# Mixture-of-experts blocks: gate and up columns side by side in one 512-column product, inner weights in pieces by halves of the rows

## The chip, the cores and the metric

The kernel runs on one core of one Trainium2 chip. The metric is device time in microseconds (us), the median over several executions. One further execution is recorded by the hardware profiler; its trace is what is read here.

## The reference

The input x is 2048 tokens of 1024 float32 numbers. A layer of convolution and state-space mixing comes first, and then a mixture of experts, cut here to what the change touches:

```
h = rms_norm(x, g_ffn)
# each token picks 1 of 4 groups, and in it 2 of 8 experts, with two gate values
for each block of 128 (token, expert) assignments of one expert e:
    hid = silu(xblk @ w_gate[e]) * (xblk @ w_up[e])      # 128x1024 @ 1024x512, twice
    y   = hid @ w_down[e]                                # 128x512  @ 512x1024
    out[token] += gate * y
```

There are 32 experts; each has its assignments padded to whole blocks of 128. The last step is a normalisation of the sum.

## The kernel before

The stages run one after the other: input projection, convolution and state space, mixing with the router, experts, final norm. The change lies in the experts' stage alone, in `ExpertWeights` and `experts`.

**Blocks.** The loops are dynamic: an outer one over the 32 experts e, an inner one over the blocks j of the expert (`over_blocks`, L1819 and the lines after it). With the inputs used there are 46 blocks. Each of the five engines runs its own copy of both loops and reads the counts from on-chip memory at each new expert. Every engine executes its instructions in program order; they are tied together by semaphores only.

**Weights.** Every product is made in three parts, for float32-like precision on TensorE: with a high and a low part of both operands, hi*hi + lo*hi + hi*lo. An expert's weights come in six pieces of 128x2048 (1 MB each). In the kernel before they are G0, U0 (gate and up for the first 256 hidden units, all 1024 rows), G1, U1 (the same for the other 256), D0, D1 (down). A piece is loaded by SyncE into `raw`, rounded by ScalarE into `hi` (`split_hi`, L1633), and subtracted by VectorE into `lo` (`split_lo`, L1637). Each of the three buffers holds one expert. The split of expert e + 1 is done during the last block of expert e (the `If(j == last - 1)` branch), each piece after the products that read the old one; the order is written out by hand in the two `body` functions of ScalarE and VectorE. In the last expert nothing is split, so 31 blocks hold a split.

**A block on TensorE** (`body` of the tensor engine), in order: `hidden` G0, U0, G1, each 8 row chunks of 3 products of 256 columns; `turn_hidden(b, 0)`, two transposes of the first half of the hidden values (L2045), which wait for VectorE's `join(b, 0)`; `hidden` U1; `turn_x(b + 1)`, eight transposes of the next block's input (L2029); `down(b, 0, 0)`, six products of 512 columns, which wait for the low part of the hidden values (`hid_low(b, 0)`, L1961); `turn_hidden(b, 1)`; three more `down`.

**Half k of the hidden values** goes through ScalarE `silu` (L1897), VectorE `join` (L1956, reads the up columns in PSUM), TensorE `turn_hidden`, ScalarE `hid_high` (L1901), VectorE `hid_low`. ScalarE's `scale_y` (L1906) takes the block's result out of PSUM, and GpSimd adds it to memory by an indirect DMA (L1879). Before `scale_y`, ScalarE waits for the block's slots `ids_s`, which GpSimd loads (L1873) once the scatter of the block before has landed.

In PSUM, gate half 0 and up half 1 share one bank (`p_g0u1`).

Of the kernel before, what the change touches and what calls it, by code (L numbers as in the profile page):

```python
# [13 lines left out]
P = 128  # L14
# [7 lines left out]
NE = NG * EPG  # L22
# [1586 lines left out]
G0, U0, G1, U1, D0, D1 = range(6)  # L1609


class ExpertWeights:
# [27 lines left out]
    def inner(self, part, u, c):  # L1640

        return part[:, u, c * 256:(c + 1) * 256]
# [130 lines left out]
def experts(nc, scratch, ident, routing, weights):  # L1773
# [7 lines left out]
    with ExitStack() as ctx:  # L1781
# [8 lines left out]
        p_g0u1, p_u0, p_g1, p_hid = ps("p_g0u1"), ps("p_u0"), ps("p_g1"), ps("p_hid")  # L1790
        p_gate = [p_g0u1[:, 0:H], p_g1[:, 0:H]]
        p_up = [p_u0[:, 0:H], p_g0u1[:, H:2 * H]]
# [17 lines left out]
        gate_done, up_done, sil_done, hid_done = (sem(n) for n in ("gate_done", "up_done", "sil_done", "hid_done"))  # L1810
# [78 lines left out]
        def _(act):  # L1889
# [5 lines left out]
            def silu(b, k):  # L1895
                act.wait_ge(gate_done, b * 2 + k + 1)
                nc.scalar.activation(sil[:, k * H:(k + 1) * H], p_gate[k], ACT.Silu).then_inc(sil_done, 1)  # L1897
# [17 lines left out]
            def body(b, e, j, last):  # L1915
                with act.If(j == last - 1):
                    silu(b, 0)
                    weights.split_hi(act, e + 1, G0)
                    act.wait_ge(up_done, b * 2 + 1)
                    weights.split_hi(act, e + 1, U0)  # L1920
                    silu(b, 1)
                    hid_high(b, 0)
                    weights.split_hi(act, e + 1, G1)
                    turn_x(b + 1)
                    hid_high(b, 1)
                    weights.split_hi(act, e + 1, U1)
                    act.wait_ge(ids_s_in, b * 16 + 16)
                    for i in range(2):
                        scale_y(b, i)
                    weights.split_hi(act, e + 1, D0)  # L1930
                    weights.split_hi(act, e + 1, D1)
                with act.Else():
                    silu(b, 0)
                    silu(b, 1)
                    hid_high(b, 0)
                    turn_x(b + 1)
                    hid_high(b, 1)
                    act.wait_ge(ids_s_in, b * 16 + 16)
                    for i in range(2):
                        scale_y(b, i)  # L1940
# [3 lines left out]
        def _(dve):  # L1944
# [8 lines left out]
            def join(b, k):  # L1953
                dve.wait_ge(sil_done, b * 2 + k + 1)
                dve.wait_ge(up_done, b * 2 + k + 1)
                V.tensor_tensor(hid[:, k * H:(k + 1) * H], p_up[k],  # L1956
# [47 lines left out]
            def body(b, e, j, last):  # L2004
                with dve.If(j == last - 1):
                    join(b, 0)
                    weights.split_lo(dve, V.tensor_tensor, e + 1, G0)
                    weights.split_lo(dve, V.tensor_tensor, e + 1, U0)
# [4 lines left out]
                    for u in (G1, U1, D0, D1):  # L2013
# [10 lines left out]
        def _(pe):  # L2024
# [7 lines left out]
            def hidden(out, e, u, done):  # L2032

                pe.wait_ge(w_lo, e * weights.PIECES + (u + 1))
                for c in range(KD):
                    w_hi, w_low = weights.inner(hi, u, c), weights.inner(lo, u, c)
                    nc.tensor.matmul(out, xh[:, c], w_hi, start=c == 0, stop=False)  # L2037
                    nc.tensor.matmul(out, xl[:, c], w_hi, start=False, stop=False)  # L2038
                    last_mm = nc.tensor.matmul(out, xh[:, c], w_low, start=False, stop=c == KD - 1)  # L2039
                last_mm.then_inc(done, 1)  # L2040
# [28 lines left out]
            def body(b, e, j, last):  # L2069
                pe.wait_ge(x_lo, b * 2 + 2)  # L2070
                wait(pe, hid_done, b * 2)
                hidden(p_gate[0], e, G0, gate_done)
                hidden(p_up[0], e, U0, up_done)
                hidden(p_gate[1], e, G1, gate_done)
                turn_hidden(b, 0)
                pe.wait_ge(sil_done, b * 2 + 1)
                hidden(p_up[1], e, U1, up_done)
# [104 lines left out]
```

## Time and profile before

| | |
|---|---|
| median of 3 runs | 1887.34 us (1884.49 to 1889.06) |
| the profiled execution's own time | 1895.12 us |
| its span, first to last instruction | 1893.7 us |
| mean granted TensorE clock | 0.924 |
| TensorE busy, share of the span | 1640.9 us, 87% |
| VectorE, ScalarE, GpSimd | 59%, 42%, 32% |

The span is 1.4 us shorter than the time of the same execution. Busy time of TensorE is a sum of modelled ends of pipelined instructions, so two starts that follow each other tell more than a duration does. PE stands for matmuls, PEld for the loads of the stationary operand, DVE for VectorE, ACT for ScalarE, POOL for GpSimd, SP for SyncE. A row of the timeline gives start, length, engine, line, what is written from what, the number of merged instructions, and in brackets the idle time of the engine before it and what ended it; "issue" is idle time that no shown wait explains.

### The profile page before, as it was taken

To read this page: it belongs to the slowest core of one execution; us is meant where nothing else is said; L and a number is where in the kernel's file an instruction comes from. 1 tells how busy PE (TensorE), PEld (TensorE's weight loads), DVE (VectorE), ACT (ScalarE), POOL (GpSimd) and SP (SyncE) were. 2 spreads that over 40 slices of the span, in tenths; PEclk is the share of its full clock that TensorE was granted. 3 is DMA by queue.
4 is the path that set the end of the run, shared out by engine and by line. 5 is a ranking of instruction groups with operands and counts; after the bars stand their busy time and mean duration, and the time that the engine had idled before them with its cause. 6 is when DMAs were issued, how large, how long until landed. Compare 5 with 4: busy or idle time off the path is not lost. (4 is left out here: it accounts for less than half of the span.)

```text
span 1893.7 us, 33245 instructions
## 1 busy us (share of the span) xinstructions
PE 1640.9 (87%) x11171; PEld 1500.2 (79%) x11172; DVE 1116.7 (59%) x1707; ACT 803.3 (42%) x1022; POOL 605.9 (32%) x882
## 2 busy tenths in 40 slices
PE   7699999688937999999269999999999999999970
PEld 7599999577827888888268999899999888989860
DVE  7845564244547566665617646654666886665546
ACT  3222221012245333342315646644665775665543
POOL 0776774222323336444311212121222121212120
PEclk9899999878968898989579999999999999999995
DMA  8544342498854224312539878885877999887749
GB/s 278 169 146 147 127 161 85 121 223 247 225 200 137 97 89 134 101 67 90 215 119 316 275 240 272 274 285 188 291 273 257 382 366 359 280 275 254 261 137 366
DMA packets 166974, 403.90 MB, mean 213 GB/s; under 512 B 67967, under 2 KB 103169, under 8 KB 140417
## 3 DMA queue, kind: packets, MB, share of 16 engines
q1 hardware_dynamic: 140320, 336.26, 49.7%
q0 software_dynamic: 20080, 58.34, 12.7%
q10 hardware_dynamic: 6512, 8.51, 1.4%
q8 instruction: 36, 0.59, 0.1%
q14 instruction: 26, 0.21, 0.0%
HBM read 313.92 MB, written 89.13 MB: 213 GB/s over the span
## 5 line engine op out<-in xcount | busy, mean ns | idle before, releaser
L1637 DVE TENSOR_TENSOR expert_lo<-expert_raw,expert_hi 128x2048 fp32r<-128x2048 f32 x192 | 430.5, 2284 | 46.4 <-ACT expert_hi L1633 44.6
L1633 ACT CAST expert_hi<-expert_raw 128x2048 fp32r<-128x2048 f32 x192 | 361.6, 1910 | 18.1 <-DMA expert_raw<-in_experts 9.8
L720 PE MATMUL proj_p_z<-proj_x_hi,proj_w_hi 128*128 128x256 f32 x768 | 222.2, 289 | 14.1 <-DVE proj_x_lo L553 14.1
L721 PE MATMUL proj_p_z<-proj_x_lo,proj_w_hi 128*128 128x256 f32 x768 | 218.7, 285 | 0.0
L722 PE MATMUL proj_p_z<-proj_x_hi,proj_w_lo 128*128 128x256 f32 x768 | 218.5, 285 | 0.0
L2037 PE MATMUL moe_p_g0u<-expert_hi,moe_xh 128*128 128x256 f32 x736 | 210.8, 286 | 1.5 <-DVE moe_xl L1950 1.5
L2039 PE MATMUL moe_p_g0u<-expert_lo,moe_xh 128*128 128x256 f32 x736 | 206.6, 281 | 0.0
L2038 PE MATMUL moe_p_g0u<-expert_hi,moe_xl 128*128 128x256 f32 x736 | 206.6, 281 | 0.0
L2052 PE MATMUL moe_p_y<-expert_hi,moe_hh 128*128 128x512 f32 x368 | 153.4, 417 | 13.1 <-DVE moe_hl L1961 13.1
L1879 POOL DMA_INDIRECT residual<-moe_y,moe_ids_s x46 | 78.5, 1708 | 265.6 <-ACT moe_y L1906 258.1
L720 PEld LDWEIGHTS proj_p_z<-proj_x_hi,proj_w_hi 128*128 128x128 f32 x768 | 148.9, 194 | 14.2 <-issue 14.1
L721 PEld LDWEIGHTS proj_p_z<-proj_x_lo,proj_w_hi 128*128 128x128 f32 x768 | 149.0, 194 | 0.1
L722 PEld LDWEIGHTS proj_p_z<-proj_x_hi,proj_w_lo 128*128 128x128 f32 x768 | 148.7, 194 | 0.0
L2053 PE MATMUL moe_p_y<-expert_lo,moe_hh 128*128 128x512 f32 x368 | 145.2, 395 | 0.0
L2037 PEld LDWEIGHTS moe_p_g0u<-expert_hi,moe_xh 128*128 128x128 f32 x736 | 139.6, 190 | 4.0 <-issue 1.9
L2038 PEld LDWEIGHTS moe_p_g0u<-expert_hi,moe_xl 128*128 128x128 f32 x736 | 140.7, 191 | 2.0
L2039 PEld LDWEIGHTS moe_p_g0u<-expert_lo,moe_xh 128*128 128x128 f32 x736 | 139.7, 190 | 0.0
L1956 DVE TENSOR_TENSOR moe_hid<-moe_p_u,moe_sil 128x256 f32<-128x256 f32 x46 | 19.5, 424 | 172.6 <-PE moe_p_u L2039 135.9
L1873 POOL DMA_DIRECT2D moe_ids_s<-slot_table x46 | 25.8, 561 | 283.2 <-DMA residual<-moe_y,moe_ids_s 276.9
L2055 PE MATMUL moe_p_y<-expert_hi,moe_hl 128*128 128x512 f32 x368 | 115.8, 396 | 0.0
L1563 PE MATMUL mix_p_out<-mix_wo_hi,mix_cat_hi 128*128 128x512 f32 x256 | 107.4, 419 | 0.0
L1564 PE MATMUL mix_p_out<-mix_wo_hi,mix_cat_lo 128*128 128x512 f32 x256 | 105.8, 413 | 0.0
(416 smaller groups left out, 4149.9 us busy)
## 6 DMA issues: line engine op xcount, KB each, us to landing
expert_raw<-in_experts SPq DMA_DIRECT2D x192, 1024.0 KB, 6.2
ffn_input<-mix_h SPq DMA_DIRECT2D x17, 512.0 KB, 3.9
proj_x_sb<-in_x SPq DMA_DIRECT2D x8, 1024.0 KB, 7.3
mix_x_sb<-in_x SPq DMA_DIRECT2D x16, 512.0 KB, 5.0
residual<-mix_x SPq DMA_DIRECT2D x16, 512.0 KB, 2.7
out<-final_x SPq DMA_DIRECT2D x16, 512.0 KB, 6.4
proj_x_raw<-in_x_turned SPq DMA_DIRECT2D x7, 1024.0 KB, 4.8
proj_w_raw<-in_w_in SPq DMA_DIRECT2D x8, 768.0 KB, 7.3
```

The lines of the kernel that those rows point to most:

```text
L720: nc.tensor.matmul(o, whi, x_hi[:, half, c], start=start, stop=False)
L721: nc.tensor.matmul(o, whi, x_lo[:, half, c], start=False, stop=False)
L722: return nc.tensor.matmul(o, wlo, x_hi[:, half, c], start=False, stop=stop)
L1563: nc.tensor.matmul(o[:, :], cat_hi[:, par, k, ts], wo_hi[:, k, sl], start=c == 0, stop=False)
L1633: self.nc.scalar.copy(self.hi[:, u], self.raw[:, u]).then_inc(self.hi_done, 1)
L1637: tensor_tensor(self.lo[:, u], self.raw[:, u], self.hi[:, u].bitcast(FP32), ALU.subtract).then_inc(self.lo_done, 1)
L2037: nc.tensor.matmul(out, xh[:, c], w_hi, start=c == 0, stop=False)
L2038: nc.tensor.matmul(out, xl[:, c], w_hi, start=False, stop=False)
L2039: last_mm = nc.tensor.matmul(out, xh[:, c], w_low, start=False, stop=c == KD - 1)
L2052: nc.tensor.matmul(p_y[i][:, :], hh[:, c], w_hi, start=c == 0, stop=False)
L2053: nc.tensor.matmul(p_y[i][:, :], hh[:, c], w_low, start=False, stop=False)
L2055: last_mm = nc.tensor.matmul(p_y[i][:, :], hl[:, c], weights.outer(hi, D0 + i, c), start=False, stop=c == F // P - 1)
```

## The change

Inner weights are laid out anew on the host: piece A0 holds, for the first 256 hidden units, gate beside up (512 columns) for rows 0 to 511, A1 the same for rows 512 to 1023; B0 and B1 are the same for the other 256 units. D0 and D1 stay. `hidden` for half k writes gate and up of that half into one PSUM bank, with products of 512 columns, and is done after both pieces. One semaphore, `inner_done`, replaces `gate_done` and `up_done`. The orders of ScalarE and VectorE are changed with it, and TensorE's wait for `sil_done` goes.

```
-G0, U0, G1, U1, D0, D1 = range(6)
+A0, A1, B0, B1, D0, D1 = range(6)
...
-    def inner(self, part, u, c):
-        return part[:, u, c * 256:(c + 1) * 256]
+    def inner(self, part, k, c):
+        return part[:, 2 * k + c // 4, (c % 4) * 512:(c % 4 + 1) * 512]
...
-        p_g0u1, p_u0, p_g1, p_hid = ps("p_g0u1"), ps("p_u0"), ps("p_g1"), ps("p_hid")
-        p_gate = [p_g0u1[:, 0:H], p_g1[:, 0:H]]
-        p_up = [p_u0[:, 0:H], p_g0u1[:, H:2 * H]]
+        p_inner, p_hid = [ps("p_inner0"), ps("p_inner1")], ps("p_hid")
...
             def silu(b, k):
-                act.wait_ge(gate_done, b * 2 + k + 1)
-                nc.scalar.activation(sil[:, k * H:(k + 1) * H], p_gate[k], ACT.Silu).then_inc(sil_done, 1)
+                act.wait_ge(inner_done, b * 2 + k + 1)
+                nc.scalar.activation(sil[:, k * H:(k + 1) * H], p_inner[k][:, 0:H], ACT.Silu).then_inc(sil_done, 1)
...
                 with act.If(j == last - 1):
                     silu(b, 0)
-                    weights.split_hi(act, e + 1, G0)
-                    act.wait_ge(up_done, b * 2 + 1)
-                    weights.split_hi(act, e + 1, U0)
+                    weights.split_hi(act, e + 1, A0)
+                    hid_high(b, 0)
+                    weights.split_hi(act, e + 1, A1)
                     silu(b, 1)
-                    hid_high(b, 0)
-                    weights.split_hi(act, e + 1, G1)
                     turn_x(b + 1)
                     hid_high(b, 1)
-                    weights.split_hi(act, e + 1, U1)
+                    weights.split_hi(act, e + 1, B0)
+                    weights.split_hi(act, e + 1, B1)
                     act.wait_ge(ids_s_in, b * 16 + 16)
...
                 with act.Else():
                     silu(b, 0)
+                    hid_high(b, 0)
                     silu(b, 1)
-                    hid_high(b, 0)
...
             def join(b, k):
                 dve.wait_ge(sil_done, b * 2 + k + 1)
-                dve.wait_ge(up_done, b * 2 + k + 1)
-                V.tensor_tensor(hid[:, k * H:(k + 1) * H], p_up[k],
+                V.tensor_tensor(hid[:, k * H:(k + 1) * H], p_inner[k][:, H:2 * H],
...
                 with dve.If(j == last - 1):
                     join(b, 0)
-                    weights.split_lo(dve, V.tensor_tensor, e + 1, G0)
-                    weights.split_lo(dve, V.tensor_tensor, e + 1, U0)
+                    weights.split_lo(dve, V.tensor_tensor, e + 1, A0)
                     hid_low(b, 0)
                     join(b, 1)
                     turn_x(b + 1)
                     hid_low(b, 1)
-                    for u in (G1, U1, D0, D1):
+                    for u in (A1, B0, B1, D0, D1):
                         weights.split_lo(dve, V.tensor_tensor, e + 1, u)
...
-            def hidden(out, e, u, done):
+            def hidden(b, e, k, rows):
 
-                pe.wait_ge(w_lo, e * weights.PIECES + (u + 1))
-                for c in range(KD):
+                pe.wait_ge(w_lo, e * weights.PIECES + (2 * k + rows[0] // 4 + 1))
+                for c in rows:
...
-                hidden(p_gate[0], e, G0, gate_done)
-                hidden(p_up[0], e, U0, up_done)
-                hidden(p_gate[1], e, G1, gate_done)
+                first, last_rows = range(KD // 2), range(KD // 2, KD)
+                hidden(b, e, 0, first)
+                hidden(b, e, 0, last_rows)
+                hidden(b, e, 1, first)
                 turn_hidden(b, 0)
-                pe.wait_ge(sil_done, b * 2 + 1)
-                hidden(p_up[1], e, U1, up_done)
+                hidden(b, e, 1, last_rows)
```

## Rows read from the trace of the kernel before

**Rows 1.** Windows, by stage: us, busy by engine, PEclk, DMA share, GB/s
```profile
core 0: us, PE busy (x) PEld busy (x) DVE busy (x) ACT busy (x) POOL busy (x), PEclk, DMA share, GB/s
965.00:1838.00 873.00, 846.11 (x6072) 784.35 (x6072) 543.45 (x463) 514.21 (x554) 178.85 (x186) 1.00 0.80 272
```

**Rows 2.** Waits, experts' stage: us in total, times, longest
```profile
DVE moe_hid L1956 <- issue: 35.1, 30, 1.7
PEld moe_p_y L2052 <- DVE expert_lo L1637: 16.9, 18, 1.0
PEld moe_p_hid L2045 <- DVE moe_hid L1956: 15.9, 25, 1.1
PE moe_p_y L2052 <- DVE moe_hl L1961: 13.1, 18, 0.8
PE moe_p_hid L2045 <- DVE moe_hid L1956: 10.9, 23, 0.9
DVE moe_hid L1956 <- ACT moe_sil L1897: 1.6, 1, 1.6
```

**Rows 3.** Timeline, TensorE, one block that begins at 1004.47
```profile
1001.67 0.40 PE L2052 MATMUL moe_p_y<-expert_hi,moe_hh 128*128 128x512 f32 x1
...
1004.47 0.28 PE L2037 MATMUL moe_p_g0u<-expert_hi,moe_xh 128*128 128x256 f32 x1
...
1012.83 0.28 PE L2039 MATMUL moe_p_g<-expert_lo,moe_xh 128*128 128x256 f32 x1
1013.83 0.44 PE L2045 MATMUL moe_p_hid<-ident,moe_hid 128*128 128x128 f32 x2 [0.72 <-DVE moe_hid L1956]
1014.02 0.36 PE L2037 MATMUL moe_p_g0u<-expert_hi,moe_xh 128*128 128x256 f32 x1
...
1016.94 1.03 PE L2029 MATMUL moe_p_x<-ident,moe_xg 128*128 128x128 f32 x8
1018.66 0.47 PE L2052 MATMUL moe_p_y<-expert_hi,moe_hh 128*128 128x512 f32 x1 [0.68 <-DVE moe_hl L1961]
```

**Rows 4.** Timeline, VectorE, the same block
```profile
1007.18 4.49 DVE L1637 TENSOR_TENSOR expert_lo<-expert_raw,expert_hi 128x2048 fp32r<-128x2048 f32 x2 [1.49 <-ACT expert_hi L1633]
1013.35 0.42 DVE L1956 TENSOR_TENSOR moe_hid<-moe_p_u,moe_sil 128x256 f32<-128x256 f32 x1 [1.68 <-issue]
1013.69 4.48 DVE L1637 TENSOR_TENSOR expert_lo<-expert_raw,expert_hi 128x2048 fp32r<-128x2048 f32 x2
1018.09 0.42 DVE L1961 TENSOR_TENSOR moe_hl<-moe_p_hid,moe_hh 128x256 fp32r<-128x256 f32 x1
...
1020.96 0.42 DVE L1961 TENSOR_TENSOR moe_hl<-moe_p_hid,moe_hh 128x256 fp32r<-128x256 f32 x1 [0.93 <-ACT moe_hh L1901]
1021.30 4.48 DVE L1637 TENSOR_TENSOR expert_lo<-expert_raw,expert_hi 128x2048 fp32r<-128x2048 f32 x2
```

**Rows 5.** Timeline, ScalarE, the same block and the start of the next
```profile
1004.67 0.69 ACT L1906 ACTIVATE moe_y<-moe_p_y,moe_ids_s 128x512 f32<-128x512 f32 x1 [0.65 <-PE moe_p_y L2055]
1005.26 3.70 ACT L1633 CAST expert_hi<-expert_raw 128x2048 fp32r<-128x2048 f32 x2
1008.86 0.37 ACT L1897 ACTIVATE moe_sil<-moe_p_g0u 128x256 f32<-128x256 f32 x1
...
1020.55 0.37 ACT L1901 CAST moe_hh<-moe_p_hid 128x256 fp32r<-128x256 f32 x1 [1.91 <-PE moe_p_hid L2045]
1020.82 1.92 ACT L1633 CAST expert_hi<-expert_raw 128x2048 fp32r<-128x2048 f32 x1
1023.41 0.69 ACT L1906 ACTIVATE moe_y<-moe_p_y,moe_ids_s 128x512 f32<-128x512 f32 x1 [0.67 <-PE moe_p_y L2055]
1024.75 0.69 ACT L1906 ACTIVATE moe_y<-moe_p_y,moe_ids_s 128x512 f32<-128x512 f32 x1 [0.65 <-PE moe_p_y L2055]
```

**Rows 6.** Timeline, TensorE, a block from 1042.85 with no wait before the down products
```profile
1054.38 1.04 PE L2029 MATMUL moe_p_x<-ident,moe_xg 128*128 128x128 f32 x8
1055.17 0.48 PE L2052 MATMUL moe_p_y<-expert_hi,moe_hh 128*128 128x512 f32 x1
```

**Rows 7.** Timeline, VectorE: the earliest `join(b, 0)` after a split
```profile
1555.01 4.49 DVE L1637 TENSOR_TENSOR expert_lo<-expert_raw,expert_hi 128x2048 fp32r<-128x2048 f32 x2 [1.50 <-ACT expert_hi L1633]
1560.17 0.42 DVE L1956 TENSOR_TENSOR moe_hid<-moe_p_u,moe_sil 128x256 f32<-128x256 f32 x1 [0.67 <-issue]
```

**Rows 8.** DMA issues, experts' stage: size, median us from issue to landing
```profile
expert_raw<-in_experts SPq DMA_DIRECT2D x180, 1024.0 KB, 6.1
moe_ids_s<-slot_table POOLq DMA_DIRECT2D x47, 1.0 KB, 3.6
residual<-moe_y,moe_ids_s POOLq DMA_INDIRECT x46, 9.1
```

**Rows 9.** Timeline, GpSimd, the block from 1493.53: scatter, load of the next slots
```profile
1495.23 1.67 POOL L1879 DMA_INDIRECT residual<-moe_y,moe_ids_s  x1 [6.28 <-ACT moe_y L1906]
1505.71 0.56 POOL L1873 DMA_DIRECT2D moe_ids_s<-slot_table  x1 [6.95 <-DMA residual<-moe_y,moe_ids_s]
```

**Rows 10.** Timeline, ScalarE: `scale_y(b, 0)` of the block from 1493.53
```profile
1512.11 0.69 ACT L1906 ACTIVATE moe_y<-moe_p_y,moe_ids_s 128x512 f32<-128x512 f32 x1 [0.68 <-PE moe_p_y L2055]
```

**Rows 11.** DMA, 1500 to 1600: GB/s in 40 slices
```profile
GB/s 200 413 423 420 382 405 416 303 188 417 433 407 416 397 413 256 218 421 426 423 416 423 426 261 297 423 426 413 415 431 393 226 377 423 420 410 397 354 295 272
```

More of the change, by code:

```diff
@@ L1809, in experts @@
         x_turned, x_hi, x_lo = sem("x_turned"), sem("x_hi"), sem("x_lo")
-        gate_done, up_done, sil_done, hid_done = (sem(n) for n in ("gate_done", "up_done", "sil_done", "hid_done"))
+        inner_done, sil_done, hid_done = sem("inner_done"), sem("sil_done"), sem("hid_done")
         hid_turned, hid_hi, hid_lo, down_done, y_done = (sem(n) for n in ("hid_turned", "hid_hi", "hid_lo", "down_done", "y_done"))
@@ L2030, in turn_x @@
                     last.then_inc(x_turned, 1)
-            def hidden(out, e, u, done):
-                pe.wait_ge(w_lo, e * weights.PIECES + (u + 1))
-                for c in range(KD):
[L2036 to L2040, printed above, removed]
+            def hidden(b, e, k, rows):
+                pe.wait_ge(w_lo, e * weights.PIECES + (2 * k + rows[0] // 4 + 1))
+                for c in rows:
+                    w_hi, w_low = weights.inner(hi, k, c), weights.inner(lo, k, c)
+                    nc.tensor.matmul(p_inner[k][:, :], xh[:, c], w_hi, start=c == 0, stop=False)
+                    nc.tensor.matmul(p_inner[k][:, :], xl[:, c], w_hi, start=False, stop=False)
+                    last_mm = nc.tensor.matmul(p_inner[k][:, :], xh[:, c], w_low, start=False, stop=c == KD - 1)
+                if rows[-1] == KD - 1:
+                    last_mm.then_inc(inner_done, 1)
             def turn_hidden(b, k):
@@ L2150 @@
     gate, up, down = (_np.asarray(inputs[n])[0] for n in ("w_gate", "w_up", "w_down"))
-    inner = [_np.ascontiguousarray(a.reshape(NE, KD, P, 2, F // 2).transpose(3, 0, 2, 1, 4)).reshape(2, NE, P, 2048)
-             for a in (gate, up)]
+    gate, up = (a.reshape(NE, KD, P, 2, F // 2).transpose(0, 3, 2, 1, 4) for a in (gate, up))
+    inner = _np.stack([gate, up], axis=4).reshape(NE, 2, P, 2, 2048).transpose(0, 1, 3, 2, 4).reshape(NE, 4, P, 2048)
     outer = _np.ascontiguousarray(down.reshape(NE, F // P, P, 2, D // 2).transpose(3, 0, 2, 1, 4)).reshape(2, NE, P, 2048)
@@ L2163 @@
     arrays["in_b_router"] = _np.concatenate([value("b_router_group"), value("b_router_expert")])
-    arrays["in_experts"] = _np.stack([inner[0][0], inner[1][0], inner[0][1], inner[1][1], outer[0], outer[1]], axis=1)
+    arrays["in_experts"] = _np.concatenate([inner, outer[0][:, None], outer[1][:, None]], axis=1)
     arrays["in_g_final"] = _np.ascontiguousarray(inputs["g_final"])
```

## The prediction

> **What bounds the kernel now.** I read the windows by stage first. From 965 to 1838 the experts run; TensorE is busy for 846 of 873 us at the full granted clock (1.00, the 2.4 GHz level) [rows 1]. It is the bound, so its idle time and the spacing of its products are what can be gained, and the waits say where it idles [rows 2]. There are two kinds. 25 blocks stop before the hidden transposes for VectorE's `join(b, 0)`, 15.9 us by the weight loads' view; 18 blocks stop before `down(b, 0, 0)` for `hid_low(b, 0)`, 16.9 us. The matmul view gives 10.9 and 13.1 for the same stops, because modelled ends of pipelined products cover the first part of a gap; spacing of starts agrees with the larger ones, so I use those. (The row names a piece's `lo` as releaser of the weight load, but in [rows 3, 4] `hid_low(0)` ends at 1018.51 and the product starts at 1018.66.)
>
> Next the timelines of one block, T = 1004.47 [rows 3 to 5]. ScalarE takes the old block's result at T+0.20, then rounds D0 and D1 until 1008.96, T+4.49. VectorE subtracts them until 1011.67, T+7.20, then does nothing for 1.68 us, with no wait that the profile can name, and starts `join(b, 0)` at T+8.88. Transposes follow 0.48 after that start. This is the passage from one block to the next: loop ends, reading of the expert's counts, the branch. Over the 31 joins behind a split the idle is 35.1 + 1.6 = 36.7 us [rows 2], 1.18 each, so the mean join starts at T+8.38; the earliest I found comes 5.16 us after the start of D0's `lo`, against 6.17 here, so at T+7.87 [rows 4, 7]. TensorE could transpose at T+8.48. The first stall is thus VectorE's lateness, set by ScalarE's D1 and the passage. The second follows from it: between `join(0)` and `hid_low(0)` VectorE does two `lo` pieces; from the join's start to `hid_low(0)`'s end are 5.16 us, and the down products start at 5.31. The 18 blocks are those with a split both in them and before them; the other 13 blocks behind a split have none of their own.
>
> **The products.** Before: 1004.47 to 1012.83 are 71 spacings, 0.1177 us each, so 72 products of 256 columns take 8.48. Products of 512 columns: twelve from 1001.67 to 1004.47, 0.2333 each [rows 3]. Gate beside up makes 36 of them before the transposes, 8.40 us, a gain of 0.08; the remaining half piece goes from 24 x 0.1177 = 2.825 to 12 x 0.2333 = 2.80, a gain of 0.025. Halving the number of products and weight loads is nearly free of effect: the columns streamed are the same. There are 46 blocks [rows 8]; the 0.08 counts in the 46 - 31 = 15 that no late join holds, 1.2 us; the 0.025 counts in all 46, 1.2 us. Sum **-2.4 us**.
>
> **The second stall goes.** VectorE now has one piece (A0), not two, between `join(0)` and `hid_low(0)`. Is A0's `hi` there? `silu(0)` must now wait for all 24 products of half 0, T+5.60 and some 0.2 for the last to end; it takes 0.27 to the next start, the rounding 1.9 [rows 5], so `hi` is there at T+8.0. The mean join starts at T+8.6 (below), A0's `lo` follows 0.34 later and gives way 2.20 after that, `hid_low` ends 0.42 later: T+11.6. `hid_high(0)` follows the transposes (T+9.1) by 0.47 and 0.37, long before. TensorE reaches the down products at 9.1 + 0.19 + 2.88 + 0.79 = T+12.9, where 0.79 is the spacing from `turn_x` in a block without the wait [rows 6]. Cover is 1.3 us, so the stall of 16.9 us goes: **-16.9 us**. If the cover fails, all of it stays.
>
> **The first stall grows.** ScalarE now rounds B0 and B1 together after `hid_high(b, 1)`, where it rounded U1 alone. In [rows 5] the old round starts at 1020.82, and `scale_y(0)` starts at 1023.41 because TensorE released it then, not ScalarE. Two roundings hand over after 3.60 (1005.26 to 1008.86), so `scale_y(0)` starts at 1024.42, `scale_y(1)` 0.59 later at 1025.01 in place of 1024.75. D0 and D1 end 0.26 later, T+4.75. VectorE has five pieces after `hid_low(b, 1)` rather than four with a gap: from 1021.30 every 2.20, D0 at 1027.90 and D1 from 1030.10 to 1032.38, T+7.83 against T+7.20. No `hi` is late for them (B1 at 1024.5, D0 at 1027.5, D1 at 1029.3).
>
> Which of the two sets the join? Either VectorE's sequencer issues D1's `lo` once D1's `hi` is done, while D0 still runs, and begins the passage then: +0.26. Or the passage counts from the end of D1's `lo`: +0.62. ScalarE's rows favour the first: `silu` of the new block starts at 1008.86, 0.10 before D1 ends, although the same passage lies between [rows 5], so control runs beside an engine instruction that is already issued. VectorE's earliest passage is 7.87 - 4.49 = 3.4 us from D1's `hi`, against 1.75 between ScalarE's D1 start and its `silu`; ScalarE must have started its passage before D1 ran. I take +0.26 and keep 0 and +0.62 as ends. 25 blocks stalled already and pay 0.26 each, 6.5 us; the 6 with a join just in time pay about 0.1 each: **+7.1 us**. One wait fewer in `join` is priced at nothing, as no row shows its cost.
>
> **Edits at nothing.** TensorE's `sil_done` wait went at once before, as `silu(0)` was over by T+4.8. In the 15 blocks not behind a split, `silu(0)` moves from T+3.0 (24 x 0.1177 and 0.2) to T+5.8 and the join to T+6.2, 2.2 us ahead of the transposes. In blocks without a split, `hid_high(0)` ahead of `silu(1)` waits for transposes that TensorE does anyway before the second half. Weights are needed at T+2.8 (A1), T+5.6 (B0), T+9.3 (B1), and are there before T, at T+1.2 and T+3.4. SyncE loads a piece once its `lo` is done. A1's load is issued near T-1.0 and its `hi` wanted at T+9.9; 6.1 us to land [rows 8] hides that.
>
> **The sum.** -2.4 - 16.9 + 7.1 = -12.2 us. The profiled execution took 1895.12, so I expect 1882.9 for such a one; it lies 7.8 over the median of the runs, 1887.34, and against that the change gives **1875.1 us**.
>
> The Trainium skill, Advanced Engine Details and Errata, section Sequencer and Instruction Queues, says that engine instructions are queued, eight deep on ScalarE and VectorE, wait for their semaphores there, and that others are read while control code runs. Taken at its word the passage would be hidden and joins would start as D1's `lo` ends. The trace disagrees on VectorE: 1.68 us idle there.
>
> **Rivals.**
> *Forecast* (0.64): as above, 1871 to 1880.
> *The passage counts from the end of D1's `lo`* (0.14). For it: the idle always lies behind that instruction; against: ScalarE. 25 x 0.62 + 6 x 0.46 = 18.3, net -1.0: 1886.3, not to be told from no change.
> *The join does not move* (0.12). The passage varies by a microsecond for the same work (T+7.87 to T+8.88), so a mean shift of 0.26 may be lost in it, or new code pass faster. Then -19.3, and with 0.02 more per block ahead of it about -20: 1867.5.
> *The passage hides wholly* (0.02): both stalls go, 16.9 + 15.9 + 2.4 = 35.2: 1852. This is what the page's rule would give.
> *DMA bunching makes it slower* (0.05). Five loads of 1.05 MB are issued 2.2 us apart, 477 GB/s, where the chip moved about 420 at best [rows 11]; before, four in a row with a gap. The backlog after five is about 1.5 us, and the scatter of y shares it. The slots for `scale_y` are loaded when the scatter lands: at 1505.71, in hand 3.6 us later [rows 8, 9], wanted at 1512.11 [rows 10], so 2.8 us are to spare. Backlog plus 0.26 stays below. Beyond 2.8, each microsecond delays D0 and D1 and the next join in 18 blocks, 18 us; slower than before from about 3.5. At 4.0 it is +21.6 - 12.2: 1896.7.
> *The second stall stays* (0.03), A0's `lo` being late by more than its 1.3 us of cover: -2.4 + 7.1 = +4.7, 1892.0.
>
> **Numbers.** Less than 0.2% (3.8 us) can't be told from no change. Faster is 0.64 + 0.12 + 0.02 = 0.78, same 0.14, slower 0.08. The range runs from the third case to the second, 1867 to 1886.5, and leaves out a tenth.
>
> **What would show it.** Stops before `down` behind a `hid_low` gone, or a few of them. Stops before the hidden transposes in all 31 blocks behind a split, some 22 us in all. `join(0)` in them at T+8.6 in the mean: at T+9.0 the second case holds, at T+8.4 the third. Products 0.233 apart with T+8.40 for 36. `scale_y(0)` released by nothing shown in blocks with a split; if a DMA releases it, the bunching holds. It would be wrong above all if the passage behaves otherwise than a fixed time behind D1's `hi`.

## The result, and the profile after

The changed kernel takes **1900.1 us** in the median of 6 runs (1894.52 to 1905.52), the kernel before 1885.03 (1882.15 to 1889.06, 6 runs). The ratio is 1.0079, with a 95% interval of 1.0060 to 1.0098: slower by 15 us, where 12 less were forecast. The profiled execution took 1899.66 us, its span is 1898.2, its mean granted clock 0.925.

The experts' stage by windows, of the changed kernel (columns as in [rows 1]):

```profile
965.00:1838.00 873.00, 839.35 (x3831) 674.41 (x3830) 546.48 (x462) 509.74 (x551) 209.78 (x181) 0.99 0.80 271
```

TensorE has 3831 products in place of 6072 and is less busy in the same stretch. The granted clock is no longer 1.00, and GpSimd is busy for 31 us more. The waits of that stage, against [rows 2]:

```profile
POOL moe_ids_s L1871 <- DMA residual<-moe_y,moe_ids_s: 317.5, 44, 10.9
...
ACT moe_y L1904 <- DMA moe_ids_s<-slot_table: 56.9, 24, 3.5
...
PEld moe_p_hid L2041 <- DVE moe_hid L1952: 45.7, 31, 4.0
...
DVE moe_hid L1952 <- issue: 12.2, 22, 1.5
```

Four things are to be seen. The stop before `down(b, 0, 0)` for `hid_low(b, 0)` (16.9 us, 18 times) is gone. The stop before the hidden transposes has grown from 15.9 to 45.7 us. A row that the kernel before does not have heads ScalarE's trouble: in 24 blocks `scale_y` waits for the block's slots. And VectorE's nameless idle time before `join` fell from 35.1 to 12.2 us, so the passage from block to block is not what grew.

DMA issues of the stage, size, median us from issue to landing, against [rows 8]:

```profile
expert_raw<-in_experts SPq DMA_DIRECT2D x180, 1024.0 KB, 8.9
...
residual<-moe_y,moe_ids_s POOLq DMA_INDIRECT x45, 11.4
```

The weight loads landed in 6.1 us before, the scatter in 9.1.

**Where the time went.** I cut each block of TensorE at four starts: block start to hidden transposes, from there to `turn_x`, to the first `down` product, to the next block. The sums run over the same 44 blocks of each kernel, from the second block's start to the last one's. The two kernels at the right come from the last experiments below: there the slots are loaded ahead, without and with the change. Each column is one traced execution.

| us, 44 blocks | before | after | slots ahead, before | slots ahead, after |
|---|---|---|---|---|
| to the hidden transposes | 385.3 | 405.4 | 387.8 | 376.3 |
| to `turn_x` | 133.7 | 143.2 | 136.1 | 134.8 |
| to `down` | 52.3 | 35.1 | 51.0 | 34.8 |
| to the next block | 259.8 | 259.8 | 260.4 | 260.8 |
| sum | 831.1 | 843.5 | 835.4 | 806.7 |

So the change made +20.1, +9.5, -17.2 and 0.0: +12.4 of the 15 us. The third row is the forecast's gain, to 0.3 us. The first is where it fails. The second is a loss for which the forecast had no term. The two traced executions as a whole differ by 4.5 us only, 1893.7 and 1898.2, because everything outside these blocks, which the change does not touch, took 1062.6 us in the one and 1054.7 in the other. Over the traces of all fourteen kernels this remainder runs from 1045.9 to 1062.6. So the sum over the blocks says more about a change in them than the time of one execution does, and it is given with the experiments below.

**One turn of the loop.** GpSimd's timeline of the changed kernel, blocks from 994.88 and 1013.12:

```profile
996.86 2.99 POOL L1877 DMA_INDIRECT residual<-moe_y,moe_ids_s  x1 [5.72 <-ACT moe_y L1904]
...
1010.76 0.55 POOL L1871 DMA_DIRECT2D moe_ids_s<-slot_table  x1 [10.29 <-DMA residual<-moe_y,moe_ids_s]
...
1017.62 1.66 POOL L1877 DMA_INDIRECT residual<-moe_y,moe_ids_s  x1 [4.58 <-ACT moe_y L1904]
```

The old block's scatter starts at T+1.98 (T = 994.88). The slots can be asked for only when it has landed; their load is issued at T+15.88. In [rows 9] that was at T+12.18. ScalarE:

```profile
1009.40 3.72 ACT L1633 CAST expert_hi<-expert_raw 128x2048 fp32r<-128x2048 f32 x2
1015.53 1.27 ACT L1904 ACTIVATE moe_y<-moe_p_y,moe_ids_s 128x512 f32<-128x512 f32 x2 [2.42 <-DMA moe_ids_s<-slot_table]
1016.69 3.72 ACT L1633 CAST expert_hi<-expert_raw 128x2048 fp32r<-128x2048 f32 x2
```

It has rounded B0 and B1 by 1013.12 and waits 2.42 us for the slots. `scale_y` runs 2.4 us into the next block, so D0 and D1 are rounded until 1020.41, T+7.3 of that block, not T+4.75. VectorE:

```profile
1009.88 6.69 DVE L1637 TENSOR_TENSOR expert_lo<-expert_raw,expert_hi 128x2048 fp32r<-128x2048 f32 x3
1018.63 4.50 DVE L1637 TENSOR_TENSOR expert_lo<-expert_raw,expert_hi 128x2048 fp32r<-128x2048 f32 x2 [2.06 <-issue]
1023.77 0.42 DVE L1952 TENSOR_TENSOR moe_hid<-moe_p_inner,moe_sil 128x256 f32<-128x256 f32 x1 [0.64 <-issue]
...
1048.90 11.09 DVE L1637 TENSOR_TENSOR expert_lo<-expert_raw,expert_hi 128x2048 fp32r<-128x2048 f32 x5
1060.08 0.43 DVE L1952 TENSOR_TENSOR moe_hid<-moe_p_inner,moe_sil 128x256 f32<-128x256 f32 x1
```

In the first block D0 comes 2.06 us late, and `join(0)` starts at T+10.65. The last two rows are a block whose slots were in time (T = 1052.14): five `lo` pieces without a gap, and the join with no idle time behind them, at T+7.94. TensorE, in the late block:

```profile
1024.25 0.44 PE L2041 MATMUL moe_p_hid<-ident,moe_hid 128*128 128x128 f32 x2 [2.56 <-DVE moe_hid L1952]
```

That block is 20.9 us long, the one before 18.24. Its own scatter was late as well, at T+4.5, so a delay is handed on to the next turn. In this kernel it does not grow there: the late scatters start in a gap of VectorE and take 1.65 to 1.80 us instead of 2.99, and the load of the slots behind them is issued at T+16.20 in the mean, against T+15.61 behind a scatter in time. A block without a split gives the time back. Of the 31 blocks behind a split, 15 have a scatter in time and a join at T+7.99 in the mean; in the other 16 the join starts at T+10.18. Over all 31 it is T+9.12.

**The clock.** After some of the long stops TensorE runs on at half speed. Products of the block from 1164.29:

```profile
1175.77 0.44 PE L2041 MATMUL moe_p_hid<-ident,moe_hid 128*128 128x128 f32 x2 [2.92 <-DVE moe_hid L1952]
...
1176.75 0.63 PE L2034 MATMUL moe_p_inner<-expert_lo,moe_xh 128*128 128x512 f32 x1
1177.17 0.63 PE L2032 MATMUL moe_p_inner<-expert_hi,moe_xh 128*128 128x512 f32 x1
...
1179.69 0.39 PE L2032 MATMUL moe_p_inner<-expert_hi,moe_xh 128*128 128x512 f32 x1
1179.92 0.40 PE L2033 MATMUL moe_p_inner<-expert_hi,moe_xl 128*128 128x512 f32 x1
```

and two windows of the same block, with the granted clock third from the end:

```profile
1150.00:1174.00 24.00, 22.85 (x104) 18.01 (x102) 19.51 (x14) 15.77 (x16) 4.91 (x5) 1.00 0.99 357
...
1176.00:1179.30 3.30, 3.30 (x10) 2.57 (x9) 0.42 (x1) 0.37 (x1) 0.00 (x0) 0.53 1.06 322
```

Starts are 0.43 us apart, then 0.23 again: the 1.2 GHz level instead of 2.4. Five blocks have it, and each loses 1.4 to 2.5 us between its transposes and `turn_x`, 8.6 us in all: most of the table's second row, +9.5 us. The stop before it is VectorE's lateness, so this too follows from the slots: with the slots loaded ahead, below, no block has it.

### The profile page after: what moved, and what is told of

The parts are those of the page before. It is cut to its first block and busy times, and to the rows that moved or that the text cites. A ratio compares the mean times of both kernels' runs of the same rounds, so it can differ in the third digit from the quotient of the medians.

```text
span 1898.2 us, 28706 instructions
## 1 busy us (share of the span) xinstructions
PE 1633.6 (86%) x8963; PEld 1390.1 (73%) x8964; DVE 1119.1 (59%) x1707; ACT 800.8 (42%) x1022; POOL 639.8 (34%) x882
## 5 line engine op out<-in xcount | busy, mean ns | idle before, releaser
L2032 PE MATMUL moe_p_inner<-expert_hi,moe_xh 128*128 128x512 f32 x736 | 299.7, 407 | 1.5 <-DVE moe_xl L1947 1.5
L2033 PE MATMUL moe_p_inner<-expert_hi,moe_xl 128*128 128x512 f32 x736 | 295.2, 401 | 0.0
L2034 PE MATMUL moe_p_inner<-expert_lo,moe_xh 128*128 128x512 f32 x736 | 294.6, 400 | 0.0
L1952 DVE TENSOR_TENSOR moe_hid<-moe_p_inner,moe_sil 128x256 f32<-128x256 f32 x92 | 39.1, 425 | 237.5 <-ACT moe_sil L1895 224.3
L1877 POOL DMA_INDIRECT residual<-moe_y,moe_ids_s x46 | 96.8, 2105 | 216.6 <-ACT moe_y L1904 213.3
L2034 PEld LDWEIGHTS moe_p_inner<-expert_lo,moe_xh 128*128 128x128 f32 x736 | 140.9, 191 | 34.4
L2032 PEld LDWEIGHTS moe_p_inner<-expert_hi,moe_xh 128*128 128x128 f32 x736 | 141.1, 192 | 34.0 <-issue 1.9
L2033 PEld LDWEIGHTS moe_p_inner<-expert_hi,moe_xl 128*128 128x128 f32 x736 | 141.2, 192 | 31.9
```

The lines of the kernel that those rows point to most:

```text
L2032: nc.tensor.matmul(p_inner[k][:, :], xh[:, c], w_hi, start=c == 0, stop=False)
L2033: nc.tensor.matmul(p_inner[k][:, :], xl[:, c], w_hi, start=False, stop=False)
L2034: last_mm = nc.tensor.matmul(p_inner[k][:, :], xh[:, c], w_low, start=False, stop=c == KD - 1)
```

## The experiments

The theories to be told apart: (A) the slots come late because VectorE's order changed and its gap closed; (B) the wide products or the new pieces do it; (C) the loads bunch up in the DMA engines; (D) the passage between blocks does it.

### First batch: the order, the width, the loads

The kernel before ran 30 times on this chip, median 1885.95 us.

**The new order in the kernel before** (products of 256 columns and the old pieces stay):

```
                     weights.split_hi(act, e + 1, G0)
+                    hid_high(b, 0)
                     act.wait_ge(up_done, b * 2 + 1)
                     weights.split_hi(act, e + 1, U0)
                     silu(b, 1)
-                    hid_high(b, 0)
-                    weights.split_hi(act, e + 1, G1)
                     turn_x(b + 1)
                     hid_high(b, 1)
+                    weights.split_hi(act, e + 1, G1)
                     weights.split_hi(act, e + 1, U1)
...
-                    weights.split_lo(dve, V.tensor_tensor, e + 1, U0)
                     hid_low(b, 0)
...
-                    for u in (G1, U1, D0, D1):
+                    for u in (U0, G1, U1, D0, D1):
```

> The order of the change on the old 256-column products: VectorE subtracts one piece before hid_low(0) and five in a row after hid_low(1); ScalarE rounds two pieces together before scale_y. Theory A (five lo pieces free five raw buffers in a row, the five 1 MB loads crowd the scatter, the slots for scale_y come late): slots late in about 20 blocks, no stall before the down products, scatter landing near 11 us, time as after the change plus 2.4 us: ratio to before 1.007 to 1.011. Theory B (the wide product does it, since silu and join come 2.8 us later in a block): no late slots, second stall gone, ratio 0.990 to 0.997.

Measured: 1905.72 us, ratio 1.0100 (1.0066 to 1.0134). Its waits:

```profile
ACT moe_y L1906 <- DMA moe_ids_s<-slot_table: 50.5, 19, 3.9
PEld moe_p_hid L2044 <- DVE moe_hid L1956: 39.5, 22, 3.6
```

The whole loss is there without one wide product, as theory A expected: 19 blocks with late slots, the scatter landing in 11.2 us, no stop before `down`. The blocks take 851.2 us, and ten of them run on at the lower clock, against 843.5 and five after the change. (B) falls: the new order is enough to bring the loss.

**The old order in the changed kernel** (VectorE subtracts A0 and A1 ahead of `hid_low(0)` and four pieces afterwards; ScalarE rounds both ahead of `hid_high(0)`):

```
-                    hid_high(b, 0)
                     weights.split_hi(act, e + 1, A1)
+                    hid_high(b, 0)
...
                     weights.split_lo(dve, V.tensor_tensor, e + 1, A0)
+                    weights.split_lo(dve, V.tensor_tensor, e + 1, A1)
                     hid_low(b, 0)
...
-                    for u in (A1, B0, B1, D0, D1):
+                    for u in (B0, B1, D0, D1):
```

> Wide products, but VectorE subtracts A0 and A1 before hid_low(0) and four pieces after hid_low(1), as the old order did; ScalarE rounds A0 and A1 before hid_high(0). Theory A: loads spread as before, no late slots, scatter landing 9 to 10 us, both stalls as before give or take 7 us: ratio 0.997 to 1.003. Theory B: late slots as after the change, ratio 1.006 or more.

Measured: 1896.05, ratio 1.0052 (1.0027 to 1.0077): missed, it is not back at the time of before. Slots are late in 5 blocks only (4.2 us), but a stop before `down` has come back, and in 29 blocks (24.3 us) rather than 18, presumably since `silu(0)` and with it A1's rounding start later than in the kernel before; 22.2 us go before the transposes. In sum the blocks take 840.7 us, two of them with the clock down. This order does not fit these pieces, and the run says little about the slots beyond their count.

**A1's subtraction put back between `hid_low(0)` and `join(1)`**, so that four pieces follow `hid_low(1)`, as before the change:

```
                     hid_low(b, 0)
+                    weights.split_lo(dve, V.tensor_tensor, e + 1, A1)
                     join(b, 1)
...
-                    for u in (A1, B0, B1, D0, D1):
+                    for u in (B0, B1, D0, D1):
```

> The changed kernel with A1's lo moved from behind hid_low(1) to between hid_low(0) and join(1): four in a row, no piece more ahead of hid_low(0). Theory A: no late slots and no stall before the down products, so what I had forecast for the change or better: ratio 0.988 to 0.995. Theory B: late slots stay, 1.005 or more.

Measured: **1878.10, ratio 0.9963** (0.9942 to 0.9985), 22 us below the changed kernel by one line. Loads landed in 7.6 us, scatters in 10.4, slots were late in 14 blocks, 11.7 us in all, and no stop before `down` came back. The blocks take 818.9 us, 24.6 less than after the change. So the run of five pieces is what hurt. The expected 0.988 to 0.995 was missed, and so was "no late slots". The waits show a second reason, a price of this order:

```profile
ACT moe_y L1904 <- DMA moe_ids_s<-slot_table: 11.7, 14, 2.9
PEld moe_p_hid L2042 <- DVE moe_hid L1952: 35.3, 62, 2.1
```

TensorE stops 62 times for a join, not 31. `join(1)` now comes behind A1's subtraction, so the transposes of the second half wait too, 0.3 us in each of the 31 blocks that hold a split, 9.2 us in all.

**Half of the load traffic**: from the second expert on, only the left half of each piece is loaded. The right half keeps the first expert's weights, so half of the loads is left out; all other instructions are the same.

```
-        engine.dma_start(self.raw[:, u], self.source[e][u]).then_inc(self.raw_in[u], 16)
+        full = isinstance(e, int) and e == 0
+        n = 2048 if full else 1024
+        engine.dma_start(self.raw[:, u, 0:n], self.source[e][u][:, 0:n]).then_inc(self.raw_in[u], 16)
```

> The changed kernel, but from the second expert on only the left half of each weight piece is loaded (work left out: the right half keeps the first expert's weights). Theory A: the scatter lands in 8 us or less, no late slots, stalls before the transposes near 0 to 10 us instead of 45.7: ratio 0.980 to 0.992. Theory B, or any cause in the order of ScalarE and VectorE alone: late starts stay, ratio 1.005 or more.

Measured: 1886.60, ratio 1.0003 (0.9980 to 1.0027), 13.5 us below the changed kernel. No slots were late and no clock fell. The scatter landed in 10.0 us, where 8 or less had been expected, and the gain stopped well short as well: the blocks take 835.2 us, and what they gain on the changed kernel's 843.5 is the clock alone (134.6 us from the transposes to `turn_x`; up to the transposes it is 406.1, no less than the 405.4 there). The reason is one that I had not seen: VectorE's passage took longer. Its timeline (T = 1147.47, the block behind the five pieces), in which the 1.25 us stand where 1052.14 above had none:

```profile
1144.22 11.09 DVE L1639 TENSOR_TENSOR expert_lo<-expert_raw,expert_hi 128x2048 fp32r<-128x2048 f32 x5
1156.56 0.43 DVE L1954 TENSOR_TENSOR moe_hid<-moe_p_inner,moe_sil 128x256 f32<-128x256 f32 x1 [1.25 <-issue]
```

and its waits:

```profile
PEld moe_p_hid L2043 <- DVE moe_hid L1954: 46.3, 31, 1.7
DVE moe_hid L1954 <- issue: 40.3, 31, 1.5
```

All 31 joins are late, by 1.3 us and evenly, at T+8.9 to T+9.4. GpSimd's rows of the same kernel matter for what follows:

```profile
1131.07 1.67 POOL L1879 DMA_INDIRECT residual<-moe_y,moe_ids_s  x1 [5.48 <-ACT moe_y L1906]
...
1149.44 2.99 POOL L1879 DMA_INDIRECT residual<-moe_y,moe_ids_s  x1 [5.72 <-ACT moe_y L1906]
```

The scatter's instruction takes 3 us with half of the traffic too, if VectorE subtracts beside it, and 1.67 where it doesn't. So 1.33 us of the slots' delay are not a matter of how much the loads move. As for (D): the passage is what keeps this kernel slow, but in the changed kernel it takes less idle time than before the change (12.2 us against 35.1), so it is not what made that one slower.

### Second batch: the slots, and the two loads

The kernel before: 1883.90 us, 19 runs.

**A second tile for the slots**, loaded one block ahead; GpSimd copies it to `ids_s` once the scatter has landed. The same edit in the changed kernel, in the kernel before, and in the one with A1 in the middle:

```
-                pool.dma_start(ids_s[:, :], table[e * MAXB + j]).then_inc(ids_s_in, 16)
+                pool.wait_ge(ids_n_in, b * 16 + 16)
+                nc.gpsimd.tensor_copy(ids_s[:, 0:1], ids_n[:, 0:1]).then_inc(ids_s_in, 8)
+                nc.gpsimd.tensor_copy(ids_s[:, 1:2].bitcast(FP32), ids_n[:, 1:2].bitcast(FP32)).then_inc(ids_s_in, 8)
+                pool.wait_ge(ids_s_in, b * 16 + 16)
+                pool.sem_inc(gathers, 1)
+                pool.dma_start(ids_n[:, :], table[row_of(b + 1)]).then_inc(ids_n_in, 16)
```

> The changed kernel, with the next block's slots loaded into a second small tile while nothing waits for them, and copied by GpSimd once the scatter of the block before has landed; so the slots' own DMA no longer lies between that landing and scale_y. Theory A (slots late, which delays scale_y, the roundings of D0 and D1, the join and TensorE): hardly any late slots, joins near T+8.0 to 8.2, no stretch with the TensorE clock halved: ratio 0.985 to 0.995, 10 to 28 us under before. Rival (the late joins come from the longer chains on ScalarE and VectorE themselves): joins stay at T+9 in the mean, ratio above 1.002.

> Control: the same second tile in the kernel before. Its slots were never late, so both theories give no change: 0.998 to 1.002. If it gains much, the staging does something beyond the slots.

> The second slot tile together with A1's lo ahead of join(1). If slots are what is left in the run with A1's lo moved alone (0.9963, 14 late slots), this reaches 0.985 to 0.993. If what is left there is VectorE's passage between blocks, it stays at 0.994 to 0.998.

Measured: 1879.85 in the changed kernel (ratio 0.9980, 0.9959 to 1.0001), 1892.10 in the kernel before (1.0054, 1.0033 to 1.0075), 1864.95 in the third (0.9911, 0.9881 to 0.9941). Only the third fell where it was expected (0.985 to 0.993); the changed kernel gained less than expected (0.985 to 0.995), and the kernel before should have stayed within 0.998 to 1.002. A load less on the path of the slots is worth 20 us to the changed kernel and costs the kernel before 8. GpSimd and VectorE in the changed kernel with this edit:

```profile
1010.40 0.18 POOL L1874 COPY moe_ids_s<-moe_ids_n 128x1 int32<-128x1 int32 x1 [9.32 <-DMA residual<-moe_y,moe_ids_s]
1010.53 2.27 POOL L1875 COPY moe_ids_s<-moe_ids_n 128x1 f32<-128x1 f32 x1
1010.48 11.09 DVE L1637 TENSOR_TENSOR expert_lo<-expert_raw,expert_hi 128x2048 fp32r<-128x2048 f32 x5
...
1031.65 0.18 POOL L1874 COPY moe_ids_s<-moe_ids_n 128x1 int32<-128x1 int32 x1 [3.23 <-DMA residual<-moe_y,moe_ids_s]
1031.79 0.17 POOL L1875 COPY moe_ids_s<-moe_ids_n 128x1 f32<-128x1 f32 x1
```

A copy of 128x1 takes 0.17 us, or up to 2.33 when a `lo` piece (2.28 us) runs on VectorE. So this edit pays GpSimd's stall a second time. In the kernel before it makes slots late that were not:

```profile
ACT moe_y L1914 <- POOL moe_ids_s L1877: 19.0, 6, 3.2
```

In the changed kernel 16 blocks still wait for the copy (24.5 us), and in 11 TensorE waits for the next input `xg` (9.5 us), whose gather GpSimd now issues behind the copies.

**The loads of D0 and D1 put off** until the next expert's A0 is subtracted, so that three loads follow each other, not five:

```
-                for u in range(weights.PIECES):
-                    sp.wait_ge(w_lo, e * weights.PIECES + (u + 1))
-                    weights.load(sp, e + 1, u)
+                for u in (A0, D0, D1, A1, B0, B1):
+                    if u in (D0, D1):
+                        weights.load(sp, e, u)
+                    else:
+                        sp.wait_ge(w_lo, e * weights.PIECES + (u + 1))
+                        weights.load(sp, e + 1, u)
```

> The changed kernel, orders of all compute engines untouched; SyncE issues the loads of D0 and D1 only after the next expert's A0 has been subtracted, so three loads in a row meet the scatter, not five. Theory A1 (five loads crowd the scatter): landing of the scatter from 11.4 back to about 9.5 us, few late slots: ratio 0.988 to 0.998. Theory A2 (VectorE, which now subtracts without a gap while GpSimd prepares the scatter, makes GpSimd slow: 3.0 us against 1.66): landing improves by less than half, late slots stay in 10 blocks or more: ratio 1.000 to 1.007.

Measured: 1892.56, ratio 1.0048 (1.0027 to 1.0069), 7.5 us below the changed kernel, with intervals that overlap. The scatter lands in 10.8 us (11.4 without the edit). Its waits:

```profile
PEld moe_p_hid L2048 <- DVE moe_hid L1959: 49.8, 31, 4.1
ACT moe_y L1911 <- DMA moe_ids_s<-slot_table: 24.6, 17, 2.0
```

This is what theory A2 expected: the landing improves by 0.6 us, less than half of what it had lost, and slots stay late in 17 blocks. The stops before the transposes did not shrink, and the traced blocks take 847.2 us, 3.7 more than in the changed kernel, so the lower time does not come from them. (C) is a part of the delay all the same: from the scatter's start to the issue of the slots' load 12.70 us pass in blocks with nothing late, where the changed kernel has 13.64 and the kernel before 10.56.

### Third batch: the delay made on purpose, and taken away

The kernel before: 1885.11 us, 17 runs.

**A late scatter in the kernel before**: GpSimd fills an unused tile ahead of each scatter. Nothing else is changed.

```
+                for i in range(7):
+                    nc.gpsimd.memset(pad[:, i], 0.0).then_inc(padded, 1)
+                pool.wait_ge(padded, b * 7 + 7)
+                pool.sem_inc(scatters, 1)
                 nc.gpsimd.indirect_dma_start(out=scratch["acc"][:, :],
```

> The kernel before, with seven fills of an unused tile (128x512 each) on GpSimd ahead of every scatter, some 3.5 us more if nothing is in their way. Nothing else is changed. Theory (a late scatter alone brings the syndrome, with 256-column products and the old orders): slots late by 1 to 3 us in most blocks that hold a split and follow one, stalls before the hidden transposes from 15.9 to over 40 us, ratio 1.008 to 1.025. Rival (the slack of 2.8 us that I worked out is larger, or what hurt was the orders): below 1.003.

Measured: 2001.88, ratio **1.0639** (1.0595 to 1.0683): the right direction, several times the size. Its GpSimd rows (T = 997.91) and its waits:

```profile
998.95 3.33 POOL L1881 MEMSET moe_pad<- 128x512 f32 x7 [4.79 <-ACT moe_y L1911]
1003.10 3.56 POOL L1884 DMA_INDIRECT residual<-moe_y,moe_ids_s  x1 [0.82 <-POOL moe_pad L1881]
...
1016.02 0.55 POOL L1874 DMA_DIRECT2D moe_ids_s<-slot_table  x1 [8.73 <-DMA residual<-moe_y,moe_ids_s]
```

```profile
ACT moe_y L1911 <- DMA moe_ids_s<-slot_table: 168.4, 38, 9.2
...
PEld moe_p_hid L2050 <- DVE moe_hid L1961: 87.8, 22, 7.8
```

The fills take 3.33 us, their wait 0.82, and they move the scatter out of VectorE's gap, so its own instruction grows from 1.66 to 3.56: 6 us in place of the 3.3 of the fills. Here the delay does grow from turn to turn: this scatter starts at T+5.19, the next one at T+11.20, and blocks reach 27 us. Fifteen blocks run on at the lower clock, which is 0.907 in the mean. No edit to the other engines is needed to lose 117 us: the slots' path alone does it.

**The slots ahead, without GpSimd's copies**: the next block's slots and weights are loaded right behind the scatter. ScalarE itself waits for the scatter's landing, copies the slots, and scales out of the new tile.

```
                 nc.gpsimd.indirect_dma_start(out=scratch["acc"][:, :],
...
+                pool.dma_start(ids_n[:, :], table[row_of(b + 1)]).then_inc(ids_s_in, 16)
...
-                                     scale=ids_s[:, 1:2].bitcast(FP32)).then_inc(y_done, 1)
+                                     scale=ids_n[:, 1:2].bitcast(FP32)).then_inc(y_done, 1)
+            def take_slots(b):
+                act.wait_ge(ids_s_in, b * 16 + 16)
+                act.wait_ge(scattered, b * 16 + 16)
+                nc.scalar.copy(ids_s[:, 0:1], ids_n[:, 0:1]).then_inc(y_done, 1)
...
-                    act.wait_ge(ids_s_in, b * 16 + 16)
+                    take_slots(b)
```

> The changed kernel with the next block's slots loaded right behind the scatter into a second tile; ScalarE itself waits for the scatter's landing, copies the ids (128x1) and scales out of that tile. Takes the slots' DMA and GpSimd out of the way without the GpSimd copies, which took up to 2.3 us. If the slots are the cause: no stall longer than about 1 us, joins at T+8.0 to 8.2, ratio 0.983 to 0.993. If not, like the changed kernel.

> The same with A1's lo ahead of join(1), which leaves the scatter a freer GpSimd and spreads the loads. Expected 0.980 to 0.990, and the best so far, below the 0.9911 of the run with the GpSimd copies.

> Control: the same slots in the kernel before, whose slots were never late: 0.998 to 1.002.

Measured: **1861.75 in the changed kernel, ratio 0.9883** (0.9856 to 0.9911), the fastest of all and within the expected 0.983 to 0.993; 1867.38 with A1 in the middle (0.9916, 0.9885 to 0.9946), which I had expected to be the best, at 0.980 to 0.990; 1890.56 in the kernel before (1.0037, 1.0015 to 1.0059), which should have stayed within 0.998 to 1.002. The first two are not told apart by their intervals; in the traces the one with A1 in the middle takes 5.9 us more in the blocks, and the stops before the second transposes, 9.0 us, are there again. The changed kernel with this edit, its waits and the scatter's landing:

```profile
PEld moe_p_hid L2046 <- DVE moe_hid L1957: 15.1, 31, 1.7
DVE moe_hid L1957 <- issue: 10.9, 31, 1.5
...
ACT moe_ids_s L1910 <- DMA moe_ids_n<-slot_table: 4.8, 9, 1.0
```

```profile
residual<-moe_y,moe_ids_s POOLq DMA_INDIRECT x46, 12.1
```

The scatter lands later than in the changed kernel (11.4), and it costs next to nothing, since no load waits for its landing: ScalarE waits 4.8 us in all. The 44 blocks take 18.2 to 18.6 us each, and none runs on at the lower clock. Against the changed kernel they save 29.1 us up to the transposes and 8.4 up to `turn_x`. With the slots out of the way the change is worth 1861.75 against 1890.56, 28.8 us faster: the table's right half. 5.5 of these us are what the edit costs the kernel before; against that kernel as it was, it is 23.4.

## Why the prediction was wrong

**The step that failed is "Backlog plus 0.26 stays below": the delay that the slots get.** The prediction had this very mechanism among its rivals: the scatter shares the DMA engines, the slots come late, D0 and D1 and the next join with them. It gave 2.8 us of slack, put a backlog of 1.5 and the rounding's 0.26 against it, and so a chance of 0.05. What was set against the slack was too small. Of the 31 blocks behind a split, take the 15 in which the scatter starts at T+2 and nothing is late yet. There the load of the slots is issued at T+15.61 in the mean, against T+12.27 in the kernel before: +3.34 us, beyond the slack by itself. 0.26 is the scatter's later start, as forecast. From its start to that issue 13.64 us pass, 10.56 before: +3.08. Of these 1.33 are its instruction (2.99 against 1.66), for which the prediction had no term: it costed what VectorE does for TensorE and left out what VectorE's idle 1.49 us (the gap before D0 in [rows 4]) had done for GpSimd. The other 1.75 lie behind the instruction, against the 1.5 estimated for the DMA engines; with half of the traffic the 13.64 are 10.96, the instruction still at 2.99. In the block from 994.88 the account closes: the issue is 3.70 us later than in [rows 9], the slots took 4.77 us to be in hand, not 3.6, and ScalarE was ready for them at T+18.24, 0.34 earlier than there, since the block is shorter. 3.70 + 1.17 + 0.34 less the slack of 2.80 is 2.41, and the trace shows a wait of 2.42.

**The price, once in, was about right for the joins and left out the clock.** It was 18 us for each microsecond beyond the slack. In the 18 blocks that hold a split and follow one, the slots held `scale_y` back by 1.8 us in the mean from where ScalarE was ready for it, 32 us in all, and with the slots loaded ahead the changed kernel gets back 29.1 us before the transposes. The clock comes on top, +8.6. The rival's 1896.7 lies within 4 us of the result, but not because its terms were right: it took 1.2 us beyond the slack for an example, it had no clock, and it started from a gain of 12.2 us that was too small.

The Trainium skill, SBUF — State Buffer, section Who interferes with whom, states that a VectorE instruction with two inputs in SBUF contends with a GpSimd instruction that reads SBUF, and not with one that only writes it, and that the loser blocks for the whole instruction. The rows agree as far as they go: the copy takes 2.27 us beside a `lo` piece of 2.28; the fills, which only write, take 3.33 though the subtractions of D0 and D1 run beside them from 1000.62 on. The same section infers that such a VectorE instruction does not stall the making of DMA descriptors; for the indirect scatter the runs here differ, 2.99 us against 1.66. I had not weighed this page.

**The second stall goes: right.** 17.2 us by the table against 16.9, and 16.2 in the pair with slots ahead. No block stops there.

**The products: right.** Twelve wide ones take 2.80, 36 of them 8.40 (T+8.40 in blocks with nothing late). In the blocks not behind a split the transposes moved from T+8.48 to T+8.40, the 0.08 of the forecast (one block of the kernel before, at T+8.17, is left aside). Halving the number of weight loads bought nothing more.

**The first stall grows: the right sign for the wrong reason.** Stops in all 31 blocks, as forecast, but 45.7 us and not 22, from late slots. ScalarE's part was as worked out: D1 rounded by T+4.8 in blocks with slots in time. But there the join came *earlier* than forecast, at T+7.99 in the mean and not T+8.6, within 0.3 us of the end of D1's `lo`. So this step failed too, to the change's advantage: the forecast counted a fixed time from D1's `hi`. The rival in which the passage hides wholly, priced at 0.02, is thus nearly true where slots are in time, and 10.9 us of idle time remain over 31 joins with slots ahead (37.0 in the kernel before with the same edit). The Trainium skill's rule (Advanced Engine Details and Errata, section Sequencer and Instruction Queues) agrees with these two kernels; the one with half of the loads, 40.3 us of idle time behind the same five instructions, disagrees. So neither "a fixed time behind D1's `hi`" nor "hidden" is a law here.

**The sum with the fault taken out.** With slots ahead: -11.5, -1.3, -16.2, +0.4, together -28.6 us where the forecast had -12.2. The second stall and the products went as forecast. The first stall shrank instead of growing, so most of the difference to the forecast is that step. One path beside them ate more than all of the gain.

**What stays open.** Why VectorE's passage takes 3.3 us from D1's rounding in some kernels and 4.2 to 4.6 in the one with half loads, with the same instructions. How the scatter's delay splits between GpSimd and the DMA engines: no kernel was run in which the one changes and the other surely doesn't. Why loading the slots ahead costs the kernel before 0.4 to 0.5%: six blocks waiting for GpSimd's copies (19.0 us) are a part of it in the first form. In both forms the transposes in blocks not behind a split come at T+8.55 instead of T+8.48, for a reason that no row shows.

## What to carry to other kernels

An idle gap of one engine can be what another needs. Before closing a gap, list what else runs in it, GpSimd's instructions and the small DMAs above all, and put their slack beside every delay that the change adds, not beside the largest one alone. A loop that holds a DMA round trip (scatter, then slots, then scale) with 3 us to spare has little margin: a delay beyond it is handed on to the next turn, and with the larger delay of the fills it grew there (from T+5.19 to T+11.20). Take the second transfer out of the loop first, and measure the change on top of that. When a rival's mechanism is certain and only its size is not, its chance is that of its size, not of a rare mishap.

## What the runs showed of the hardware that was not expected

- GpSimd's indirect scatter instruction takes 1.66 us when VectorE is in a gap at its start and 2.99 (3.56 in the kernel with the fills) beside subtractions of 128x2048; a GpSimd copy of 128x1 takes 0.17, or up to 2.33 beside them. Seven fills of 128x512 take 3.32 to 3.34 in all 46 blocks.
- Loads of 512 KB landed in 6.6 us, of 1 MB in 8.9 with the same order of instructions, and of 1 MB in 6.1 in the kernel before: the order counts for as much as the size.
- After stops of 2 to 4 us TensorE ran on at 0.43 us from product to product, with a granted clock of 0.53 in the stretch shown, in five blocks of the changed kernel, and not after others as long (the block from 1070.32 stops for 2.9 us).
- A scatter that landed in 12.1 us, later than the changed kernel's 11.4, left ScalarE waiting 4.8 us in all once no load waited for its landing, where 56.9 us of waits had been.
